# Two FFN layers on one core: the up-projection as seven half-size block products, and a down-projection that reads its input back from DRAM

## The chip, the cores and the metric

One Trainium2 chip, one of its cores. A core has TensorE (PE; its weight loads are listed as PEld), VectorE (DVE), ScalarE (ACT), GpSimd (POOL) and SyncE (SP, which only issues DMAs), each with its own in-order queue; they meet in semaphores. SBUF holds the working data in 128 partitions, PSUM is eight banks of 128 x 512 fp32, and DRAM is reached by DMA. The metric is the device time of one execution in microseconds (us); less is better.

## The reference

A two-layer encoder over 1024 prompt tokens and 256 sample tokens, all fp32, model width 1024. Layer 0 mixes tokens with a Conformer convolution, layer 1 with windowed attention; each mixer, and each FFN, is followed by a residual LayerNorm. The change touches the FFN and the normalisations on either side:

```
x = layer_norm(ALPHA * x + mix, ...)
h = depthwise_conv(x @ w_up, w_dw, b_dw)      # w_up 1024 x 5504, three taps along the tokens
g, u = split(h, 2)                             # gate and up, 2752 channels each
f = (silu(g) * u) @ w_down                     # w_down 2752 x 1024
x = layer_norm(ALPHA * x + f, ...)
```

## The kernel before

**Products.** Every fp32 operand is split into a high part (`fp32r`, a rounded copy) and a low part (what is left), and each product is three matmuls into one PSUM bank: high x high, low x high, high x low (`product`, L669, L672, L674). Weights come from DRAM in pieces of 128 x 512 (256 KB) into four slots (`raw_pieces`), and GpSimd makes both parts of each piece (L595, L599) in a ring of eight (`w_hi`, `w_lo`). A slot of the ring is written again when TensorE has used the piece that lay there.

**FFN.** The 2752 channels are 21 tiles of 128 (`FT` = 21) and a rest of 64. For each tile `up_tile(f)` computes 128 gate channels and 128 up channels in three token chunks (512, 512, 256): for each chunk and part, eight blocks of the contraction times three matmuls. So a tile is 96 matmuls of 512 columns and 48 of 256. ScalarE applies the centre tap on the way out of PSUM (L1275), VectorE the two others (L1606, L1612), ScalarE the silu (L1280), VectorE the product (L1625), and the two parts of h are made by ScalarE (L1287) and VectorE (L1639). h stays in SBUF, three tiles of it. After every second tile `down_pair(g)` multiplies the last two h tiles with their rows of `w_down`: 20 results of 128 tokens x 512, twelve matmuls for two, and VectorE adds each result to `y` in SBUF (L1645), 220 such additions a layer with the last tile and the rest. `up_rest` is the 64 + 64 left channels.

**Around it.** Before each FFN the output projection of the mixer runs in two halves of the columns, n = 0 and n = 1. While n = 1 runs token tile by token tile, VectorE adds and normalises each tile (L1568, L1393, L1406, L1411), TensorE turns it with eight transposes (L699), ScalarE makes its high part (L1130) and VectorE its low part (L1419), one tile behind another. At the end of the FFN `last_down(t)` gives each token tile its last ten matmuls, and VectorE then adds, normalises and splits the tiles one by one; in layer 0 the K and V projections stand between them, in layer 1 the tiles go out: VectorE L1700, ScalarE L1301, GpSimd L659, store by SP.

**Order.** There is no planner: each engine's program is written out, in the order of its queue.

Of the kernel before, what the change touches and what calls it, by code (L numbers as in the profile page):

```python
# [57 lines left out]
def trunk(nc, w, out_prompt, out_sample, residual_dram):  # L58
# [26 lines left out]
    GROUPS = (FT - 1) // 2  # L85
    assert 2 * GROUPS + 1 == FT and GROUPS % 2 == 0
    CONV_COLS = 2 * FT + 1

# [5 lines left out]
    UP_AT, DOWN_AT, N_FFN = [], [], 0  # L94
    for f in range(FT):
        if f >= 3 and f % 2:
            DOWN_AT.append(N_FFN)
            N_FFN += 4
        UP_AT.append(N_FFN)
        N_FFN += 4  # L100
    UP_AT.append(N_FFN)
    DOWN_AT += [N_FFN + 2, N_FFN + 6]
    N_FFN += 10
    assert len(DOWN_AT) == GROUPS + 1
    B_KV = B_FFN0 + N_FFN
    B_Q = B_KV + 8
# [3 lines left out]
    FFN_BASE = [B_FFN0, B_FFN1]  # L110

    with ExitStack() as ctx:
# [7 lines left out]
        XW = HW = T  # L120
# [6 lines left out]
        XL = sb("x_lo", [P, KT, XW], F32R)  # L127
        y = sb("y", [P, TT, D])
# [54 lines left out]
        OUT_AT = [0, HALF - 1, S0, T]  # L183
        OUT_MAX = HALF + 1
        with ExitStack() as a:
            h_first = [sb("h_hi_third", [P, HW], F32R, where=a), sb("h_lo_third", [P, HW], F32R, where=a)]
            HR = sb("h_rest", [P, HW], F32R, where=a)
            h_slot = [[sb(f"h_{part}_{i}", [P, HW], F32R, where=a) for part in ("hi", "lo")] for i in range(2)]
            g_conv = [sb(f"gate_conv{i}", [P, OUT_MAX], where=a) for i in range(2)]
            u_conv = [sb(f"up_conv{i}", [P, OUT_MAX], where=a) for i in range(2)]  # L190
            edge = sb("edge_columns", [P, 2, 2], where=a)
        HH, HL = ([h_slot[0][i], h_slot[1][i], h_first[i]] for i in range(2))
        with ExitStack() as a:
            gain = sb("gain_rows", [P, D], where=a)
            shift = sb("shift_rows", [P, D], where=a)
        with ExitStack() as a:
            sb("below_bias", [P, 3 * HW], where=a)
            pw2_bias = sb("pw2_bias_rows", [P, D], where=a)
# [52 lines left out]
        res_stored = sem("residual_stored")  # L251
# [3 lines left out]
        ffn_up = sem("ffn_up_done")  # L255
        ffn_mid = sem("ffn_centre_taps_done")
        ffn_edge = sem("ffn_edge_columns_kept")
        ffn_conv = sem("ffn_conv_done")
        ffn_gc = sem("ffn_gate_ready")
        ffn_silu = sem("ffn_silu_ready")  # L260
        ffn_prod = sem("ffn_product_ready")
        ffn_hi = sem("ffn_h_hi_ready")
        ffn_h = sem("ffn_h_ready")
# [1557 lines left out]
```

## Time and profile before

| | us |
|---|---|
| median of 3 runs | 2860.65 |
| lowest and highest of them | 2860.15, 2862.54 |
| profiled execution, first to last instruction (its span) | 2858.5 |
| TensorE busy in it | 2750.6 (96%) |
| VectorE busy | 1510.3 (53%) |
| GpSimd busy | 840.7 (29%) |
| ScalarE busy | 772.0 (27%) |

The profiled execution has no time of its own beside its span; the three runs lie 1.7 to 4.0 us above that span, the median 2.15 us. Busy time counts an engine as working from the start to the modelled end of its instructions. Matmuls overlap in the pipeline, so what a matmul costs is read from the distance between two starts and not from its own length. TensorE's granted clock was 0.988 of 2.4 GHz on average.

### The profile page before, as it was taken

The numbers are of one execution on the slowest core, as the hardware profiler recorded it, in microseconds if no ns is written. First come the engines' busy times: TensorE is split into PE (matmuls) and PEld (weight loads), VectorE is DVE, ScalarE is ACT, GpSimd is POOL, SyncE is SP. The second block draws the span as 40 slices with busy tenths as digits, with TensorE's granted clock in tenths as the row PEclk, the third lists the DMA queues.
The fourth block names the chain that finished last, engine by engine and source line by source line (L and its number), as shares of the span: only waits on it lengthen the run. The fifth ranks groups of instructions, "written<-read, shape, count | busy, mean of one in ns | idle before, by whom it ended". The sixth has DMA issues, their size and how long they took to land.

```text
span 2858.5 us, 36567 instructions
## 1 busy us (share of the span) xinstructions
PE 2750.6 (96%) x14349; PEld 2260.0 (79%) x14349; DVE 1510.3 (53%) x2542; ACT 772.0 (27%) x1791; POOL 840.7 (29%) x813
## 2 busy tenths in 40 slices
PE   8999869999999999999989999999999999999995
PEld 7887758788888888888778744778888888888884
DVE  3689865754444454434680288275444544444457
ACT  3333562221111122211221288213111222111122
POOL 3221202232232333223213166422323223232323
PEclk9999989999999999999999999999999999999998
DMA  4100003111111111111121000411111111111111
GB/s 138 30 23 22 30 1 125 30 45 34 41 45 30 45 37 41 39 33 45 58 82 45 0 1 1 152 33 37 39 36 45 37 38 37 37 45 30 45 37 74
DMA packets 158648, 124.69 MB, mean 44 GB/s; under 512 B 27906, under 2 KB 135802, under 8 KB 158489
## 3 DMA queue, kind: packets, MB, share of 16 engines
q1 hardware_dynamic: 149640, 96.83, 11.9%
q10 hardware_dynamic: 8848, 25.69, 2.5%
q8 instruction: 106, 1.74, 0.3%
q14 instruction: 54, 0.43, 0.1%
HBM read 112.01 MB, written 10.49 MB: 43 GB/s over the span
## 4 chain that ended last, share of the span: by engine, by line
PE 85%; DVE 10%; ACT 3%; issue 2%; DMA 0%; POOL 0%; POOLq 0%; DVEq 0%; ACTq 0%; SPq 0%
PE bank L669 26%; PE bank L672 25%; PE bank L674 25%; PE bank L754 3%; PE bank L1034 2%; PE bank L1050 2%; PE bank L1062 2%; DVE y L1482 2%; DVE stats L1393 1%; DVE y L1411 1%; ACT y L1244 1%; DVE y L1406 1%; DVE x_lo L1419 1%; DVE y L1645 1%; PE bank L699 1%
## 5 line engine op out<-in xcount | busy, mean ns | idle before, releaser
L669 PE MATMUL bank<-x_hi,w_hi 128*128 128x512 f32 (+1 forms) x2688 | 959.8, 357 | 3.7 <-DVE x_lo L1419 1.6
L674 PE MATMUL bank<-x_hi,w_lo 128*128 128x512 f32 (+1 forms) x2688 | 952.5, 354 | 0.0
L672 PE MATMUL bank<-x_lo,w_hi 128*128 128x512 f32 (+1 forms) x2688 | 952.3, 354 | 0.0
L595 POOL CAST w_hi<-raw_pieces 128x512 fp32r<-128x512 f32 x348 | 246.6, 709 | 1823.4 <-issue 1260.6
L669 PEld LDWEIGHTS bank<-x_hi,w_hi 128*128 128x128 f32 x2688 | 509.1, 189 | 90.3 <-issue 9.6
L674 PEld LDWEIGHTS bank<-x_hi,w_lo 128*128 128x128 f32 x2688 | 508.9, 189 | 71.0
L672 PEld LDWEIGHTS bank<-x_lo,w_hi 128*128 128x128 f32 x2688 | 509.3, 189 | 69.9
L599 POOL TENSOR_TENSOR w_lo<-raw_pieces,w_hi 128x512 fp32r<-128x512 f32 x348 | 469.4, 1349 | 27.9
L1645 DVE TENSOR_TENSOR y<-y,bank 128x512 f32<-128x512 f32 x440 | 296.2, 684 | 195.7 <-PE bank L674 193.8
L1606 DVE SCALAR_TENSOR_TENSOR gate_conv<-bank,ffn_conv_table,gate_conv 128x510 f32<-128x510 f32 x132 | 86.2, 653 | 372.9 <-ACT up_conv L1275 370.9
L669 PE MATMUL bank<-w_hi,h_hi 128*128 128x512 f32 x560 | 218.2, 390 | 3.3 <-DVE y L1645 3.3
L672 PE MATMUL bank<-w_lo,h_hi 128*128 128x512 f32 x560 | 218.0, 389 | 0.0
L674 PE MATMUL bank<-w_hi,h_lo 128*128 128x512 f32 x560 | 217.9, 389 | 0.0
L1482 DVE SCALAR_TENSOR_TENSOR y<-glu,conv_table,y 128x1024 f32 (+3 forms) x266 | 215.6, 883 | 0.1
L1270 ACT ACTIVATE edge_columns<-bank 128x2 f32<-128x2 f32 x86 | 14.8, 173 | 718.2 <-PE bank L674 718.2
L669 PE MATMUL bank<-w_hi,x_hi 128*128 128x512 f32 (+1 forms) x400 | 150.8, 377 | 17.3 <-DVE x_lo L1543 9.1
L1602 DVE SCALAR_TENSOR_TENSOR gate_conv<-edge_columns,ffn_conv_table,gate_conv 128x2 f32<-128x2 f32 x44 | 11.7, 265 | 266.4 <-ACT up_conv L1275 264.6
L1280 ACT ACTIVATE gate_conv<-gate_conv 128x511 f32<-128x511 f32 (+1 forms) x132 | 74.2, 562 | 283.3 <-DVE gate_conv L1612 270.0
L674 PE MATMUL bank<-w_hi,x_lo 128*128 128x512 f32 (+1 forms) x400 | 147.9, 370 | 0.0
L672 PE MATMUL bank<-w_lo,x_hi 128*128 128x512 f32 (+1 forms) x400 | 147.8, 369 | 0.0
L669 PEld LDWEIGHTS bank<-w_hi,h_hi 128*128 128x128 f32 x560 | 105.2, 188 | 25.5 <-issue 4.1
L674 PEld LDWEIGHTS bank<-w_hi,h_lo 128*128 128x128 f32 x560 | 105.1, 188 | 21.9
(175 smaller groups left out, 3416.2 us busy)
## 6 DMA issues: line engine op xcount, KB each, us to landing
raw_pieces<-in_ffn_w_up_dram SPq DMA_DIRECT2D x168, 256.0 KB, 2.8
raw_pieces<-in_ffn_w_down_dram SPq DMA_DIRECT2D x84, 256.0 KB, 2.6
raw_pieces<-in_conv_w_pw_dram SPq DMA_DIRECT2D x48, 256.0 KB, 2.7
y<-in_x_prompt_dram ACTq DMA_DIRECT2D x16, 512.0 KB, 7.0
residual_dram<-y ACTq DMA_DIRECT2D x10, 512.0 KB, 2.6
y<-residual_dram ACTq DMA_DIRECT2D x10, 512.0 KB, 12.2
out_dram<-y SPq DMA_DIRECT2D x10, 512.0 KB, 2.6
raw_pieces<-in_attn_w_q_dram SPq DMA_DIRECT2D x32, 128.0 KB, 2.4
```

Source lines behind the costliest of these rows:

```text
L595: pool.tensor_copy(WH[:, p % RING, :], raw[:, p % RAW, :]).then_inc(piece_hi, 1)
L599: pool.tensor_tensor(WL[:, p % RING, :], raw[:, p % RAW, :], WH[:, p % RING, :].bitcast(F32), ALU.subtract).then_inc(piece_split, 1)
L669: mm = pe.matmul(out, left[0], right[0], start=first, stop=False)
L672: pe.matmul(out, left[0], right[1], start=False, stop=False)
L674: return pe.matmul(out, left[1], right[0], start=False, stop=last)
L754: mm = pe.matmul(bank[b + h][:, 0:n], diagonals[left][rows], right[rows, at:at + n], start=(first and m == 0), stop=(last and m == 2))
L1034: pe.matmul(bank[SCORE_BANKS[q % 3]][:, 0:len(kb) * P], q_sb[half, GROUP * rr + s // 2, cols(n)], k_sb[half, rr, kb[0] * P:(kb[-1] + 1) * ...
L1050: mm = pe.transpose(bank[PROBS_BANKS[u % 3]][:, cols(r)], probs_of(i)[:, 2 * r + par, c0:c0 + P], ident[:])
L1280: act.activation(gb[0:rows, 0:n], gb[0:rows, 0:n], ACT.Silu).then_inc(ffn_silu, 1)
L1482: ins = dve.scalar_tensor_tensor(out=out, in0=glu[:, c, a0 + k:a0 + k + n], scalar=tap(k), in1=out, op0=ALU.mult, op1=ALU.add)
L1606: dve.scalar_tensor_tensor(out=bufs[part][:, to], in0=bank[2 * (s % 2) + part][:, at], scalar=tab(0, part), in1=bufs[part][:, to], op0=ALU ...
L1645: dve.tensor_tensor(y[:, t, half], y[:, t, half], bank[4 + m % 4][:], ALU.add).then_inc(down_kept, 1)
```

## The change

**Up-projection.** For the 1024 prompt tokens, each tile of 128 gate and 128 up channels is now a 2 x 2 block product. The left blocks are A11, A12 (tokens 0 to 511, first and second half of the 1024 inputs) and A21, A22 (tokens 512 to 1023); the right blocks are B11, B21 (gate) and B12, B22 (up). It is computed with seven products in place of eight: A11 B11, A12 B21, S2 T2, S3 T3, S1 T1, A22 T4, S4 B22, each of twelve matmuls of 512 columns. The S are sums of the token blocks, made once a layer by GpSimd in rows of `y` (`row_sums`, `last_row_sum`), then turned by TensorE in 32 "cells" of four transposes, with a high part by ScalarE and a low part by VectorE per cell. The T are sums of weight pieces, four additions a tile on VectorE (`weight_sums`). The seven products go to banks X, Y and W; between them ScalarE copies a bank out while the same bank goes on accumulating, and VectorE adds the rest (`sum_c11`, `sum_c22`, `sum_c21`). The 256 sample tokens are computed as before.

**h.** The convolution, silu and product now run on whole rows of 1280 tokens, and h goes to DRAM in fp32, one store a tile from ScalarE's queue.

**Down-projection.** After all tiles the down-projection runs for token tiles 0-3, 4-6 and 7-9 in turn. Each of these groups goes through all 22 steps of h and `w_down`, summed in PSUM, so `w_down` is loaded and split three times and VectorE adds to `y` 20 times a layer. The normalisation of one group stands beside the steps of the next.

**Splits.** In the FFN the high part of a weight piece is now made by ScalarE, the low part by GpSimd. The residual rows go to DRAM before the FFN and come back inside the down-projection.

The core of the diff:

```diff
+    ROLES = 8
+    D_GROUPS = [(0, 4), (4, 7), (7, TT)]
+    D_BANKS = [(4, 3, 2, 0, 7, 5, 1, 6), (4, 3, 2, 0, 5, 1), (4, 3, 2, 0, 5, 1)]
+    H_STEPS = FT + 1
+    H_RING = 4
...
+        h_dram = nc.dram_tensor("h_dram", (H_STEPS, P, T), F32, kind="Internal").ap()
...
+            def row_sums(layer, j):
+                pool.wait_ge(ln_ready, ln + j + 5)
+                pool.wait_ge(res_stored[j + 4], done)
+                pool.tensor_tensor(a21, a21, a22, ALU.add).then_inc(sums_ready, 1)
+                pool.wait_ge(res_stored[j], done)
+                pool.wait_ge(cell_turned, CELLS * layer + 2 * j + 2)
+                pool.tensor_tensor(a11, a21, a11, ALU.subtract).then_inc(sums_ready, 1)
+                pool.tensor_tensor(a12, a12, a11, ALU.subtract).then_inc(sums_ready, 1)
...
+                for j in range(3):
+                    row_sums(layer, j)
+                role_low(layer, 0, 0)
+                role_low(layer, 0, 1)
+                role_low(layer, 0, 2)
+                row_sums(layer, 3)
+                role_low(layer, 0, 3)
+                role_low(layer, 0, 4)
+                for j in range(4):
+                    last_row_sum(layer, j)
...
+                    def p6():
+                        pe.wait_ge(piece_split, p + 4)
+                        pe.wait_ge(up_kept, kept + 1)
+                        block(X, p + 3, S2, False, True, more=True, uses=1, ...).then_inc(ffn_x, 1)
+                    def p5():
+                        pe.wait_ge(piece_split, p + 6)
+                        pe.wait_ge(up_kept, kept + 2)
+                        block(X, p + 5, S1X, False, True, more=True, uses=1, ...).then_inc(ffn_x, 1)
+                    def p4():
+                        pe.wait_ge(piece_split, p + 7)
+                        pe.wait_ge(up_kept, kept + 3)
+                    def p3():
+                        pe.wait_ge(piece_split, p + 8)
+                        pe.wait_ge(up_summed, summed + 2)
...
+                        for part in (up_sample_low, p1, gate_sample_low, p2, gate_sample_high, p6, p7, p5, p4, p3,
+                                     up_sample_high):
+                            part()
...
+                def down_step(g, f):
+                    pe.wait_ge(h_low, H_ALL * layer + i + 1)
+                    for n in range(2):
+                        pe.wait_ge(piece_split, p + 1)
+                        for t in range(t1 - t0):
+                            if f == 0:
+                                down_bank_free(g, u)
+                            mm = product(out, (hi[:, cols(t)], lo[:, cols(t)]), weights, f == 0, False, uses=last)
...
+                def weight_sums(f):
+                    dve.wait_ge(piece_split, done + 2)
+                    dve.tensor_tensor(b11, b12, b11, ALU.subtract).then_inc(t_ready, 1)
+                    dve.tensor_tensor(t2_sum[:], b22, b11, ALU.subtract).then_inc(t_ready, 1)
+                    dve.tensor_tensor(b12, b22, b12, ALU.subtract).then_inc(t_ready, 1)
+                    dve.tensor_tensor(b21, b21, t2_sum[:], ALU.subtract).then_inc(t_ready, 1)
-                def add_down(m, t, n):
-                    dve.wait_ge(down_done, d0 + m + 1)
-                    dve.tensor_tensor(y[:, t, half], y[:, t, half], bank[4 + m % 4][:], ALU.add
```

**ScalarE in one tile in the middle of the up-projection.** Names: `edge_columns`, `gate_conv`, `up_conv` are buffers of one chunk; `gate_rows`, `up_rows` hold the sums of products, `gate_out`, `up_out` the convolved rows, `t_sum` one of the weight sums. Before, two of the three chunks:

```order
L1270 ACTIVATE edge_columns<-bank 128x2
L1275 ACTIVATE gate_conv<-bank,ffn_conv_table 128x511
L1270 ACTIVATE edge_columns<-bank 128x2
L1275 ACTIVATE up_conv<-bank,ffn_conv_table 128x511
L1280 ACTIVATE gate_conv<-gate_conv 128x511
L1287 ACTIVATE h_hi<-up_conv 128x511
L1273 ACTIVATE gate_conv<-edge_columns,ffn_conv_table 128x1
L1275 ACTIVATE gate_conv<-bank,ffn_conv_table 128x512
```

Now, from the first product's copy on:

```order
L1561 ACTIVATE gate_rows<-bank 128x512
L1511 ACTIVATE w_hi<-raw_pieces 128x512 x2
L1557 ACTIVATE gate_out<-bank,ffn_conv_table 128x256
L1592 DMA h_dram<-up_out 128x1280
L1511 ACTIVATE w_hi<-raw_pieces 128x512
L1561 ACTIVATE gate_rows<-bank 128x512
L1511 ACTIVATE w_hi<-t_sum 128x512
L1561 ACTIVATE up_rows<-bank 128x512
L1511 ACTIVATE w_hi<-raw_pieces 128x512 x3
L1557 ACTIVATE gate_out<-gate_rows,ffn_conv_table 128x1024
L1561 ACTIVATE up_rows<-bank 128x512
```

Eight weight copies, a store and four bank copies have come into ScalarE's queue; the bank copies stand behind weight copies that wait for ring slots.

**GpSimd at the start of a layer's FFN.** Before, the pieces of the first tile only:

```order
L595 CAST w_hi<-raw_pieces 128x512 [waits raw_landed3,piece_used]
L599 TENSOR_TENSOR w_lo<-raw_pieces,w_hi 128x512 [waits piece_hi]
L595 CAST w_hi<-raw_pieces 128x512 [waits raw_landed0,piece_used]
L599 TENSOR_TENSOR w_lo<-raw_pieces,w_hi 128x512 [waits piece_hi]
L595 CAST w_hi<-raw_pieces 128x512 [waits raw_landed1,piece_used]
L599 TENSOR_TENSOR w_lo<-raw_pieces,w_hi 128x512 [waits piece_hi]
```

Now, the last of the first three row sums and on (`t2_sum` is a weight sum):

```order
L732 TENSOR_TENSOR y<-y 128x512 [waits residual_stored6,ln_ready]
L736 TENSOR_TENSOR y<-y 128x512 [waits row_sums_ready,cell_turned,residual_stored2]
L738 TENSOR_TENSOR y<-y 128x512 [waits row_sums_ready]
L718 TENSOR_TENSOR w_lo<-raw_pieces,w_hi 128x512 [waits piece_hi] x3
L732 TENSOR_TENSOR y<-y 128x512 [waits residual_stored7,ln_ready]
L736 TENSOR_TENSOR y<-y 128x512 [waits row_sums_ready,cell_turned,residual_stored3]
L738 TENSOR_TENSOR y<-y 128x512 [waits row_sums_ready]
L718 TENSOR_TENSOR w_lo<-t2_sum,w_hi 128x512 [waits piece_hi]
L718 TENSOR_TENSOR w_lo<-raw_pieces,w_hi 128x512 [waits piece_hi]
L744 TENSOR_TENSOR y<-y 128x512 [waits row_sums_ready,cell_turned] x4
```

The low parts of the first pieces now stand behind nine additions that wait for the LayerNorm of token tiles 4 to 6 and for their stores.

## Rows read from the trace of the kernel before

**Rows 1.** The page: busy time; the chain that ended last, by engine.
```profile
PE 2750.6 (96%) x14349; PEld 2260.0 (79%) x14349; DVE 1510.3 (53%) x2542; ACT 772.0 (27%) x1791; POOL 840.7 (29%) x813
PE 85%; DVE 10%; ACT 3%; issue 2%; DMA 0%; POOL 0%; POOLq 0%; DVEq 0%; ACTq 0%; SPq 0%
```
**Rows 2.** Stretches: length, busy PE, PEld, DVE, ACT, POOL (count); clock, DMA share, GB/s.
```profile
474.70:574.90 100.20, 94.82 (x466) 79.16 (x465) 75.42 (x109) 19.78 (x42) 24.54 (x23) 0.97 0.11 29
574.90:1417.20 842.30, 839.72 (x4153) 713.52 (x4154) 387.45 (x624) 166.45 (x337) 244.88 (x245) 1.00 0.14 40
1417.20:1521.60 104.40, 92.06 (x564) 80.11 (x563) 68.73 (x119) 19.41 (x45) 23.82 (x24) 0.98 0.24 77
1859.30:1958.10 98.80, 93.38 (x466) 78.09 (x464) 70.22 (x105) 19.78 (x42) 24.35 (x23) 0.98 0.11 30
1958.10:2800.70 842.60, 839.95 (x4154) 713.67 (x4155) 387.72 (x624) 166.46 (x337) 240.81 (x240) 1.00 0.14 38
2800.70:2858.50 57.80, 27.11 (x99) 19.51 (x98) 46.24 (x71) 14.34 (x20) 23.64 (x10) 0.80 0.23 91
440.00:475.00 35.00, 33.95 (x151) 27.78 (x150) 16.50 (x16) 1.94 (x2) 14.27 (x14) 1.00 0.67 240
```
**Rows 3.** TensorE's timeline: start, length, line, what; first and last of a run.
```profile
630.37 0.40 PE L669 MATMUL bank<-w_hi,h_hi 128*128 128x512 f32 x1
...
679.13 0.39 PE L674 MATMUL bank<-x_hi,w_lo 128*128 128x512 f32 x1
679.36 0.28 PE L669 MATMUL bank<-x_hi,w_hi 128*128 128x256 f32 x1
...
684.99 0.28 PE L674 MATMUL bank<-x_hi,w_lo 128*128 128x256 f32 x1
...
552.10 1.04 PE L699 MATMUL bank<-ident,y 128*128 128x128 f32 x8
552.89 0.47 PE L669 MATMUL bank<-x_hi,w_hi 128*128 128x512 f32 x1
```
**Rows 4.** Groups by form: count, busy us, mean ns; idle before, releaser.
```profile
L599 POOL TENSOR_TENSOR w_lo<-raw_pieces,w_hi 128x512 fp32r<-128x512 f32 x348 | 469.4, 1349 | 27.9
L1645 DVE TENSOR_TENSOR y<-y,bank 128x512 f32<-128x512 f32 x440 | 296.2, 684 | 195.7 <-PE bank L674 193.8 <-PE bank L967 1.8
L1419 DVE TENSOR_TENSOR x_lo<-bank,x_hi 128x512 fp32r<-128x512 f32 x80 | 51.6, 686 | 69.7 <-ACT x_hi L1130 69.6
L1130 ACT ACTIVATE x_hi<-bank 128x512 fp32r<-128x512 f32 x80 | 43.2, 590 | 42.4 <-PE bank L699 42.4
L1625 DVE SCALAR_TENSOR_TENSOR up_conv<-gate_conv,up_conv 128x511 f32<-128x511 f32 x42 | 29.1, 692 | 5.0 <-ACT gate_conv L1280 0.5
```
**Rows 5.** TensorE's timeline behind an idle stretch.
```profile
542.11 1.97 PE L699 MATMUL bank<-ident,y 128*128 128x128 f32 x8 [4.71 <-DVE y L1411]
...
544.30 0.63 PE L672 MATMUL bank<-x_lo,w_hi 128*128 128x512 f32 x1
...
548.14 0.44 PE L672 MATMUL bank<-x_lo,w_hi 128*128 128x512 f32 x1
```
**Rows 6.** Timeline of VectorE and GpSimd: the same operations beside each other and alone.
```profile
539.96 2.09 DVE L1411 SCALAR_TENSOR_TENSOR y<-y,rstd,shift_rows 128x1024 f32<-128x1024 f32 x1
547.65 1.29 DVE L1411 SCALAR_TENSOR_TENSOR y<-y,rstd,shift_rows 128x1024 f32<-128x1024 f32 x1
538.85 2.12 POOL L599 TENSOR_TENSOR w_lo<-raw_pieces,w_hi 128x512 fp32r<-128x512 f32 x1
```
**Rows 7.** Timeline: GpSimd's last additions before the last store.
```profile
2850.83 4.64 POOL L659 TENSOR_TENSOR y<-y,shift_rows_end 128x1024 f32<-128x1024 f32 x2 [2.47 <-ACT y L1301]
```
**Rows 8.** DMA issues: what, queue, count, KB each, median us to landing.
```profile
raw_pieces<-in_ffn_w_down_dram SPq DMA_DIRECT2D x84, 256.0 KB, 2.6
residual_dram<-y ACTq DMA_DIRECT2D x10, 512.0 KB, 2.6
y<-residual_dram ACTq DMA_DIRECT2D x10, 512.0 KB, 12.2
```

More of the change, by code:

```diff
@@ L127, in trunk @@
         XL = sb("x_lo", [P, KT, XW], F32R)
+        with ExitStack() as a:
+            gate_out = sb("gate_out", [P, T], where=a)
+            up_out = sb("up_out", [P, T], where=a)
+            sb("below_sample", [P, 3 * D - 2 * T], where=a)
+            SMP = pair("sample", [P, KT, T - 2 * HALF], a)
         y = sb("y", [P, TT, D])
@@ L636, in normalise_part, with low, role_low @@
                 ins.then_inc(probs_ready_pool, 1)
-            def ffn_stretch(first, end):
-                for p in range(first, end):
-                    split(p, landed(p), p - RING + 1)
-                    split_low(p, p + 1)
+            def low(p, source):
+                pool.wait_ge(piece_hi, p + 1)
+                pool.tensor_tensor(WL[:, ring(p), :], source, WH[:, ring(p), :].bitcast(F32), ALU.subtract
+                                   ).then_inc(piece_split, 1)
+            def role_low(layer, f, j):
+                low(FFN_BASE[layer] + ROLES * f + j, role_source(RAW_BASE[layer] + 4 * f, j))
@@ new lines, in ffn, with block @@
+                x0, y0, w0, s0 = UPS_X * layer, UPS_Y * layer, UPS_W * layer, UPS_S * layer
+                kept0, summed0, cells0 = KEPT_ALL * layer, SUMMED_ALL * layer, CELLS * layer
+                tiles0 = FT * layer
+                def block(out, p, x, start, stop, uses=0, between={}, k0=0, more=False):
+                    for k in range(QUARTER):
+                        between.get(k, lambda: None)()
+                        mm = product(out, wblock(p, k), (x[0][:, k0 + k, :], x[1][:, k0 + k, :]),
+                                     start and k == 0, stop and k == QUARTER - 1, uses=uses and k == QUARTER - 1,
+                                     more=more)
+                    between.get(QUARTER, lambda: None)()
+                    return mm
@@ L982, in _ @@
+                for f in range(FT):
+                    sections(f)
+                rest()
+                for g in range(3):
+                    for f in range(H_STEPS):
+                        if layer == 0 and g >= 1 and f - 1 in LN_AT:
+                            t = D_GROUPS[g - 1][0] + LN_AT.index(f - 1)
+                            if t < D_GROUPS[g - 1][1]:
+                                turn_tile(1, t)
+                        down_step(g, f)
             unit = 0
@@ L1093, in _ @@
             out_projection(B_O, 1)
-            last_down = ffn(1, 3)
-            for t in range(TT):
-                last_down(t)
+            ffn(1)
         @block.scalar
```

1170 lines of the change are left out of this document (785 added, 385 removed).

## The prediction

> **What bounds the kernel now.** I read the page first: TensorE is busy for 96% of the span and carries 85% of the chain that ended last [rows 1]. So the time is the number of matmuls times the distance between two of them, plus the stretches in which TensorE waits. Then the stretches [rows 2]. In the two long ones, from the second up-tile of a layer to `last_down` (842.3 and 842.6 us), TensorE hardly waits. In the short ones it does: 10 to 17 us where a layer's FFN begins or ends, and 35 us at the very end, where PE is busy for 27.11 of 57.80. Last the timeline for the distances [rows 3]: 216 matmuls of 512 columns start from 630.37 to 679.13, 0.2268 us each; 48 of 256 columns from 679.36 to 684.99, 0.1198 each; eight transposes take 0.79.
>
> I write one block (4 x 3 matmuls of 512 columns) as 2.72 us. An up-tile before is 96 x 0.2268 + 48 x 0.1198 = 27.5 us.
>
> The sum is made against the span of the profiled execution, 2858.5 us. The median of the runs is 2.15 us above it, and I add that at the end.
>
> **1. The long stretches: 12 matmuls fewer a tile.** Seven blocks of twelve for gate and up over 1024 tokens in place of eight: an up-tile becomes 84 x 0.2268 + 48 x 0.1198 = 24.8 us. The rest of 64 channels (48 + 24 matmuls, 13.8 us) and the down-projection (1200 matmuls up to the last step's hundred, 272.2 us) keep their number. One long stretch had 20 x 27.5 + 13.8 + 272.2 = 836.4 us of work in 842.3. It will have 20 x 24.8 + 286.0 = 782.0.
>
> What hides the other engines' work in a tile of 24.8 us:
> - GpSimd: eight low parts at 1.35 = 10.8 [rows 4]; the high parts have gone.
> - ScalarE: eight weight copies and four bank copies at 0.59, then by the same rate per column three pieces of 1024 to 1280 columns and two of 256: about 12.
> - VectorE: four weight sums, three bank sums (0.69 each), two taps on 1023 columns for gate and up (some 1.3 each, as L1411 alone [rows 6]), sample taps, the product: about 14. The 220 additions into `y` (L1645, 0.684 [rows 4]) shrink to 20.
>
> None comes near 24.8, so the order within the queues decides. The tightest link: bank X is copied by ScalarE after S2 T2, and the next product into X, S1 T1, comes one block (2.72) later. ScalarE's queue holds nothing there that waits for anything later, and the copy takes 0.6, so some 1.9 us are spare. The same holds for W (A22 T4), and for the VectorE sum before S4 B22. Of the weight copies behind them each waits for a slot that TensorE frees one block later, and the piece it makes is wanted a tile afterwards. So I charge no wait a tile. If that cover goes, each of 40 tiles pays (rival A).
>
> Down-projection: a step is 24 matmuls (5.44 us) for four token tiles and 18 (4.08) for three. It needs two low parts from GpSimd (2.7), three copies from ScalarE (1.8), two weight pieces and one of h by DMA. ScalarE and GpSimd run up to three and a half steps ahead (ring of eight pieces, four of h). In SP's queue the h load of a step, which waits for h's low part four steps back, stands before the next rows; that also lies ahead of TensorE. The traffic is 512 KB + 192 KB in 4.08 us, about 175 GB/s. The stretch 440 to 475 moved 240 GB/s at a DMA share of 0.67 while TensorE was busy for 33.95 of 35 [rows 2]. The residual's return (ten loads that took 12.2 us each when issued together [rows 8]) falls in group 0. Bounds for waits in this stretch: 0 and 20 us a layer; before it was 6. I take 4, as it was nearly so before: 786.0.
>
> Two stretches: 1684.9 becomes 1572.0, **-112.9**.
>
> **2. Where a layer's FFN begins.** From the start of the n = 1 half to the second up-tile: 100.2 and 98.8 us [rows 2], of which 240 matmuls (54.4), the first tile (27.5) and 80 transposes (7.9) are work: 89.8. Now the first tile is 24.8, and 32 cells of four transposes are 12.6: work 91.8. The waits, from TensorE's arrival at the first product (57.6 in):
> - The low parts of pieces 0 and 1 stand behind nine row sums on GpSimd (1.3 each), the last three of which wait for the LayerNorm of token tile 6 (about 50 in; VectorE needs 4.3 for a tile, the additions and sums at 0.69 and two operations like L1411 at 1.2 to 1.3, and 1.4 for two cells) and for its store, issued only after the next tiles' deviations, 2.6 us to landing [rows 8]. They are ready at about 64.3: 6.7 us of wait.
> - The S3 cells want `last_row_sum`, behind three row sums and two low parts more: 9 x 1.3 after piece 1. TensorE arrives 4.5 us early.
> - Then VectorE paces: 24 low parts of cells (0.686 [rows 4]), two LayerNorms, seven sums, 30 us, before A22 T4 may begin. 5 us more.
> - The first pieces of the second tile wait for the end of the first: 1.
>
> Together 17. Some operations of VectorE and GpSimd stretch each other here: L1411 took 2.09 beside GpSimd and 1.29 alone, and a low part 2.12 [rows 6]. With 2 for that: 19 us of waits, where it was 10.4 and 9.0. 91.8 + 19 = 110.8, so +10.6 and +12.0: **+22.6**. Bounds: +3 a layer, if the stores and sums hide, and +25, if VectorE and GpSimd run at the stretched lengths all through.
>
> The Trainium skill ("GPSIMD Engine Reference", section Specifications) says that GpSimd's SBUF interfaces are shared with VectorE and contend when VectorE reads two SBUF inputs. By that rule the trace agrees with the 2.09 against 1.29. It speaks against this change, because the taps read `gate_rows` in SBUF now and not a bank; fully serialised, a tile would hold 10.8 + 9 us on that port, still under 24.8, so it would add nothing to a tile.
>
> **3. The end of layer 0.** 104.4 us [rows 2], with 100 matmuls of `last_down`, K and V (96 of 512, 288 of 256 columns) and 80 transposes: 86.9 of work. VectorE paced it, one LayerNorm and split after the other. Now tiles 0 to 6 are normalised beside the steps of later groups, only 7 to 9 are left, and K and V of the first chunk (19.4 us) stand before tile 7 is turned: VectorE has it by then. What is late next: in groups 1 and 2 a turned tile wants the low part of the one before, which VectorE makes within a microsecond of it. I take 3 us: 89.9, **-14.5**.
>
> **4. The end.** 57.8 us with 22.7 of matmuls. Now after the last step (2.7 us) comes for three tiles: add, statistics, gain (some 4 each), ScalarE's scale 1.15, GpSimd's addition 2.32, the last at about 19.9 from the start of that step, and 3.0 from GpSimd's end to the span's [rows 7]. So 22.7 + 20.2 = 42.9: **-14.9**.
>
> **Sum.** -112.9 + 22.6 - 14.5 - 14.9 = -119.7; 2858.5 - 119.7 + 2.15 = 2741 us.
>
> **Rivals.**
> A. The up-tile is paced by the exchange of banks between TensorE, ScalarE and VectorE. For it: three links of one block, and stretched VectorE operations [rows 6]. Against: 1.9 us spare. With 1.5 us a tile, 40 x 1.5 = 60: 2801. Chance 0.11.
>
> B. The first tile of a layer runs at the half clock. After 4.71 us idle, ten matmuls started 0.427 apart (544.30 to 548.14) [rows 5], the 1.2 GHz level, and this tile has a wait of 7 and several short ones. At that level all through, its 84 + 48 matmuls take 22.6 us more, of which some 7.6 fill waits: +15 a layer, 2771. Against: before, the full level was back at 548.4, and here the matmuls are dense between waits. Chance 0.12.
> The Trainium skill ("TensorE: Matmul & The Clock Gate", section What's actually happening) has the half rate as the default, released by activity; the rows 5 agree, and the rule would keep a stop-and-go tile slow.
>
> C. Slower than before: the down-projection is paced by its loads and splits. If the four raw slots and SP's order let only one step's pair be on its way, a step takes 2.6 (landing) + 0.6 + 2 x 1.35 + 0.4 = 6.3 us: 88 steps at +2.2 and 44 at +0.9 give 233: 2974. It outweighs the gain from 5.44 us a step in the groups of three, 132 GB/s. Against it: 240 GB/s in rows 2. Chance 0.05.
>
> D. The start hides as well as before (+3 a layer) and the long stretches have no wait: 2741 - 17 - 8 = 2716 to 2724. Chance 0.10.
>
> The forecast itself has 0.62, with 2728 to 2756 as its own range. That the change doesn't do what it says (more matmuls than counted) is excluded by the count of the blocks.
>
> The range, 2714 to 2802, reaches to D and A and leaves out C and what lies beyond these two. About 0.2% (6 us) is what a measurement can tell from no change. Faster 0.94, same 0.01, slower 0.05.
>
> **What would show it.** Right: TensorE's count down by 504 - 96 = 408; distances 0.2268 within a block; up-tiles 24.8 apart; down steps 4.08 and 5.44; no idle on TensorE beyond the layer's start. Wrong: idle time before a block with ScalarE's bank copy or VectorE's bank sum as releaser (A), granted clock under 0.9 in the first tile (B), idle before a down step with GpSimd's low part or a DMA as releaser (C).

## The result, and the profile after

The changed kernel takes 2762.8 us (median of 4 runs, 2762.3 to 2763.4) against 2860.4 (2859.8 to 2862.5) before on the same chip: 0.965 of it, with a 95% interval of 0.964 to 0.967. The forecast was 2741. The profiled execution has a span of 2761.5 us, 97.0 less than before, where the sum had 119.7.

The page of the changed kernel, busy time and the chain that ended last, beside [rows 1]:

```profile
PE 2650.4 (96%) x13941; PEld 2177.3 (79%) x13941; DVE 1524.8 (55%) x2112; ACT 1164.8 (42%) x2247; POOL 1217.5 (44%) x931
PE 86%; DVE 6%; ACT 3%; issue 2%; POOL 2%; DMA 1%; POOLq 0%; DVEq 0%; ACTq 0%; SPq 0%
```

The count of matmuls fell by exactly the 408 foreseen. GpSimd and ScalarE have half as much work again, and TensorE still carries the chain.

The same stretches as in [rows 2] (length, busy PE, PEld, DVE, ACT, POOL with counts; clock, DMA share, GB/s): a layer's FFN start, the rest up to the Q projection (two rows) or to the last matmul and the end, then a stretch of nothing but up-tiles and one of the down-projection:

```profile
476.58:593.13 116.55, 99.94 (x502) 81.25 (x500) 88.66 (x119) 31.19 (x60) 39.51 (x28) 0.96 0.19 68
593.13:1413.78 820.65, 815.50 (x4068) 692.61 (x4069) 436.74 (x472) 360.69 (x569) 430.36 (x307) 1.00 0.37 117
1413.78:1472.77 58.99, 58.99 (x409) 55.22 (x409) 19.98 (x45) 10.77 (x24) 10.67 (x12) 1.00 0.18 52
1812.37:1930.24 117.87, 100.92 (x501) 83.01 (x499) 83.77 (x115) 31.18 (x60) 38.30 (x28) 0.93 0.19 67
1930.24:2741.00 810.76, 807.10 (x4012) 685.84 (x4012) 411.52 (x452) 360.49 (x562) 429.23 (x301) 1.00 0.37 116
2741.00:2761.50 20.50, 0.00 (x0) 0.00 (x0) 10.66 (x17) 4.22 (x6) 6.99 (x3) 0.60 0.19 77
750.00:800.00 50.00, 50.00 (x267) 43.26 (x266) 28.87 (x33) 23.12 (x34) 22.61 (x16) 1.00 0.22 69
1140.00:1320.00 180.00, 178.39 (x801) 146.97 (x800) 79.70 (x79) 72.01 (x129) 108.56 (x78) 1.00 0.60 192
```

Each start is placed as in [rows 2], 16.4 us before the first eight transposes of the n = 1 half (those start at 492.94 and 1828.68 here, at 491.07 and 1875.61 before). Layer 0 from the n = 1 half to the Q projection takes 116.5 + 820.7 + 59.0 = 996.2 us, where it was 1046.9; layer 1 from the n = 1 half to the end 949.1, where it was 999.2. So 50.7 and 50.1 less. Of that the span lost 3.8 again in stretches that the change does not touch. The kernel's first batch of products took 17.0 us (17.01 to 34.02) where it took 15.0 (17.36 to 32.36), because the first of them were 0.43 apart as in [rows 5], the half clock (though the mean granted clock is given as 1.00 from 17.00 to 21.50). From the Q projection to layer 1's n = 1 half it took 339.6 us where it took 337.7; the mean granted clock from 1748 to 1753 was 0.66. Both differences are of these two profiled executions: in experiments 4, 5 and 6 the first batch took 15.0 again.

The layers themselves miss the forecast by 9.5 and 9.4 us, and most of it lies in the first row of each: 116.5 and 117.9 where 110.8 was expected.

TensorE's timeline there (start, length, line, what, idle before and releaser; layer 0, the rows with idle time), and the fifth prompt product of the second tile:

```profile
542.69 0.79 PE L803 MATMUL bank<-a_hi,w_hi 128*128 128x512 f32 x1 [7.50 <-POOL w_lo L718]
550.22 0.52 PE L848 MATMUL bank<-ident,y 128*128 128x128 f32 x3 [1.17 <-DVE s_lo L2025]
553.14 0.33 PE L848 MATMUL bank<-ident,y 128*128 128x128 f32 x1 [1.58 <-POOL y L744]
563.95 0.41 PE L848 MATMUL bank<-ident,y 128*128 128x128 f32 x2 [1.75 <-DVE s_lo L2025]
575.30 0.30 PE L848 MATMUL bank<-ident,y 128*128 128x128 f32 x1 [1.79 <-DVE a_lo L2025]
577.43 0.54 PE L803 MATMUL bank<-a_hi,w_hi 128*128 128x512 f32 x1 [1.50 <-DVE a_lo L2025]
593.13 0.39 PE L803 MATMUL bank<-sample_hi,w_hi 128*128 128x256 f32 x1 [0.81 <-POOL w_lo L718]
610.67 0.47 PE L803 MATMUL bank<-s_hi,w_hi 128*128 128x512 f32 x1 [1.97 <-ACT gate_rows L1561]
```

The seven waits up to the second tile add up to 16.1 us (16.9 in layer 1); 17 were forecast, in the same places, with 7.5 for 6.7 at the first product and 2.75 for 4.5 at the cells behind it. The stretch is 116.5 long with 91.8 of work, so 8.6 are left that no wait accounts for (9.2 in layer 1). These are matmuls further apart: the mean granted clock was 0.50 and 0.63 behind two of the waits (same columns), some 4 us in all, and the rest are fractions at 32 cells.

```profile
542.69:547.00 4.31, 4.31 (x15) 3.52 (x15) 3.76 (x3) 0.63 (x1) 4.14 (x3) 0.50 0.01 2
577.40:582.00 4.60, 4.57 (x17) 3.72 (x18) 1.17 (x2) 1.03 (x2) 0.00 (x0) 0.63 0.02 4
```

### The profile page after: what moved, and what is told of

It reads as the page before. It is cut to its first block, busy times and chain, and to the rows that moved or that the text cites. A ratio compares the mean times of both kernels' runs of the same rounds, so it can differ in the third digit from the quotient of the medians.

```text
span 2761.5 us, 37212 instructions
## 1 busy us (share of the span) xinstructions
PE 2650.4 (96%) x13941; PEld 2177.3 (79%) x13941; DVE 1524.8 (55%) x2112; ACT 1164.8 (42%) x2247; POOL 1217.5 (44%) x931
## 4 chain that ended last, share of the span: by engine, by line
PE 86%; DVE 6%; ACT 3%; issue 2%; POOL 2%; DMA 1%; POOLq 0%; DVEq 0%; ACTq 0%; SPq 0%
PE bank L803 25%; PE bank L806 25%; PE bank L808 25%; PE bank L902 3%; PE bank L1269 2%; PE bank L1285 2%; PE bank L1297 2%; DVE y L1924 2%; POOL w_lo L718 1%; ACT y L1473 1%; PE bank L833 1%; PE bank L848 1%; DVE y L1853 0%; DVE y L1848 0%; DVE stats L1834 0%
## 5 line engine op out<-in xcount | busy, mean ns | idle before, releaser
L718 POOL TENSOR_TENSOR w_lo<-raw_pieces,w_hi 128x512 fp32r<-128x512 f32 x564 | 787.9, 1407 | 737.2 <-ACT w_hi L1511 736.4
L1511 ACT ACTIVATE w_hi<-raw_pieces 128x512 fp32r<-128x512 f32 x564 | 351.3, 628 | 492.8 <-PE bank L803 414.5
L803 PE MATMUL bank<-s_hi,w_hi 128*128 128x512 f32 x680 | 268.0, 394 | 4.1 <-ACT gate_rows L1561 4.1
L806 PE MATMUL bank<-s_lo,w_hi 128*128 128x512 f32 x680 | 265.7, 391 | 0.0
L808 PE MATMUL bank<-s_hi,w_lo 128*128 128x512 f32 x680 | 265.4, 390 | 0.0
L803 PE MATMUL bank<-a_hi,w_hi 128*128 128x512 f32 x528 | 211.6, 401 | 18.0 <-POOL w_lo L718 15.0
L803 PE MATMUL bank<-x_hi,w_hi 128*128 128x512 f32 (+1 forms) x624 | 226.0, 362 | 1.6 <-DVE x_lo L1861 1.6
L808 PE MATMUL bank<-x_hi,w_lo 128*128 128x512 f32 (+1 forms) x624 | 221.5, 355 | 0.0
L806 PE MATMUL bank<-x_lo,w_hi 128*128 128x512 f32 (+1 forms) x624 | 221.3, 355 | 0.0
L806 PE MATMUL bank<-a_lo,w_hi 128*128 128x512 f32 x528 | 208.9, 396 | 0.0
```

Of the source, the lines that this page charges most:

```text
L718: pool.tensor_tensor(WL[:, ring(p), :], source, WH[:, ring(p), :].bitcast(F32), ALU.subtract).then_inc(piece_split, 1)
L803: mm = pe.matmul(out, left[0], right[0], start=first, stop=False, skip_group_check=more)
L806: pe.matmul(out, left[0], right[1], start=False, stop=False, skip_group_check=more)
L808: return pe.matmul(out, left[1], right[0], start=False, stop=last, skip_group_check=more)
L1511: act.activation(WH[:, ring(base + p), :], source, ACT.Copy).then_inc(piece_hi, 1)
```

## The experiments

All are edits of the changed kernel. Times are compared with its 2762.8, ratios with the kernel before on the chip of the run (for the changed kernel 0.9652).

**1. Eight blocks again**

```diff
-                        block(X, p + 7, S4, False, True, more=True).then_inc(ffn_x, 1)
+                        block(X, p + 7, S4, False, False, more=True)
+                        block(X, p + 7, S4, False, True, more=True).then_inc(ffn_x, 1)
```

> Each of the 21 up-tiles of a layer repeats its last prompt block, S4 B22, once more: 12 matmuls of 512 columns, so eight blocks a tile as before the change; loads, splits, copies and sums stay (h is then not the reference's). It takes back the term of the long stretches alone. My theory (TensorE bounds every tile, a block is 2.72 us): up-tiles 27.5 apart, +57.1 a layer, 2762.8 + 114 = 2877, TensorE still without idle time in the tiles. Rival 1 (TensorE is not all that paces the tiles; some of the saved block is filled by waits of other engines): less than +2.4 a tile, under 2863. Rival 2 (the wait at the fourth product of the second tile is hidden by the longer tile): 4 less, 2873.

Measured: 2874.9 us, ratio 1.0043 (1.0029 to 1.0057), 112 us more for 42 blocks; 2.67 a block. TensorE's sample products of two tiles stand 27.6 apart (708.32 and 735.90). No tile in the middle of the up-projection waits. The block is the whole gain: without it, the new structure is slower than the old one by 0.4%. The rows say where: in the changed kernel the two starts are 35.4 us longer than before, although each saves a block too, and the rest of the two layers is 27 us shorter than the saved blocks alone would make it.

**2. How far off the next bound is**

```diff
+                if two_pass[0]:
+                    return mm2
                 return pe.matmul(out, left[1], right[0], start=False, stop=last, skip_group_check=more)
```

> In the up-tiles from the second on and in the down-projection each product is two matmuls instead of three (high x low is left out, so the output is not the reference's); everything that other engines do stays. It shows how far off the next bound is. By count an up-tile would be 56 x 0.2268 + 32 x 0.1198 = 16.5 us, a down step 3.63 (four token tiles) and 2.72 (three). My theory: the up-tile follows TensorE down to 17 to 19 (GpSimd has 8 low parts at 1.35 to 1.41 = 11.3, VectorE 14.3, ScalarE 11.5 in it), the down steps of three stop at about 3.0, where GpSimd's two low parts (2.7 to 2.9) and 704 KB a step (the loads) are. Rival A (the exchange of banks or the copies pace the tile close under 24.8): 22 or more a tile. Rival C (the down-projection is near its bound by loads and splits): steps of three over 3.8, idle TensorE with a DMA or GpSimd as releaser.

Measured: 2465.4 us (one run). Up-tiles came 19.65 apart (first A11 B11 matmul at 659.33, 678.94, 698.64) with 16.5 of work. TensorE's timeline shows the two waits of a tile:

```profile
689.62 0.47 PE L804 MATMUL bank<-s_hi,w_hi 128*128 128x512 f32 x1 [1.27 <-ACT gate_rows L1568]
692.98 0.47 PE L804 MATMUL bank<-a_hi,w_hi 128*128 128x512 f32 x1 [1.28 <-ACT up_rows L1568]
```

and the timelines of VectorE and ScalarE what stands before them:

```profile
685.84 1.97 DVE L2119 SCALAR_TENSOR_TENSOR up_out<-gate_out,up_out 128x1280 f32<-128x1280 f32 x1
687.91 0.56 ACT L1564 ACTIVATE gate_out<-bank,ffn_conv_table 128x256 f32<-128x256 f32 x1 [4.53 <-DVE up_out L2119]
```

ScalarE waits 4.5 us for VectorE's product of the last tile, and the copies of banks stand behind that. So the next bound of an up-tile is the chain VectorE, ScalarE, bank, at 19.6 us, 5 under the 24.8 of TensorE. Rival A had the right place and the wrong distance. In the down-projection, steps of three token tiles ran at 2.72 in layer 0's group 1 (no idle in six steps from 1159.93 on); in layer 1 some waited 0.7 to 2.1 for GpSimd's low parts, where a GpSimd addition of 2.4 to 2.7 stood between. Layer 1's last group as a whole took 3.3 us a step (2370.28 to 2439.30, 21 steps). TensorE also waited up to 7.5 us for a turned tile in layer 0 and 8.8 at a change of group. A step of 4.08 is thus still clear of rival C, but by less than 2.72 says.

**3. Short row sums, and short low parts in layer 0's down-projection**

```diff
-                pool.tensor_tensor(a21, a21, a22, ALU.add)
+                pool.tensor_tensor(a21[:, 0:8], a21[:, 0:8], a22[:, 0:8], ALU.add)
...
+                pool.tensor_tensor(WL[:, ring(p), 0:8], raw[:, slot, 0:8], WH[:, ring(p), 0:8].bitcast(F32),
+                                   ALU.subtract).then_inc(piece_split, 1)
```

> Two edits in stretches that are apart. (1) GpSimd's 16 row sums a layer work on 8 columns instead of 512 (the S blocks are then not the reference's). (2) In layer 0's down-projection GpSimd's low parts are made for 8 columns only. Theory (the row sums in front of the first pieces' low parts are the wait of 7.5 us at the first product, and GpSimd stretches VectorE's operations with two SBUF inputs): the wait of 7.5 shrinks to under 2, the stretch from the n = 1 half to the second tile from 118 to 105 to 110 in both layers, so 2738 to 2748 in all; VectorE's low parts of h (128x384, 1.30 us on average) become about 0.5 in layer 0 and stay in layer 1. Rival (first tile is set by VectorE's chain of cells, LayerNorms and weight sums, or by the low clock): under 4 us a layer, 2755 or more; rival for (2): 1.30 is the operation's own length, and it stays in layer 0.

Measured: 2741.1 us, ratio 0.9575 (0.9559 to 0.9591), 21.8 us less. The first wait is 2.5 instead of 7.5, and the mean granted clock from 534 to 560 was 1.00 in place of 0.87. From the end of the n = 1 half to the second tile it took 48.6 us in place of 58.3, in layer 1 50.1 in place of 59.7. So the row sums cost 9.7 us a layer in that stretch. They are not the whole 21.8: from the fourth tile to the Q projection layer 0 was 3.4 us shorter, where its four waits of 0.8 had gone (three for a turned tile, one at a change of group). That belongs to the second edit, the short low parts. In layer 0's start no matmul ran at the half clock here, and 4.0 us still are neither work nor wait; that is the price of the handovers at the cells alone.

VectorE's low parts of h (by form, layer 0's groups of three while the down-projection ran) in the changed kernel, and then here in layer 0 and in layer 1:

```profile
L2124 DVE TENSOR_TENSOR h_lo<-h_raw,h_hi 128x384 fp32r<-128x384 f32 x42 | 55.2, 1314 | 78.4 <-ACT h_hi L1537 78.4
```

```profile
L2132 DVE TENSOR_TENSOR h_lo<-h_raw,h_hi 128x384 fp32r<-128x384 f32 x42 | 23.4, 558 | 114.0 <-ACT h_hi L1545 114.0
...
L2132 DVE TENSOR_TENSOR h_lo<-h_raw,h_hi 128x384 fp32r<-128x384 f32 x42 | 53.3, 1270 | 91.6 <-ACT h_hi L1545 91.6
```

The operation itself takes 0.56 us; beside GpSimd's full low parts it takes 1.3.

**4. The first wait filled with matmuls**

```diff
+                            for i in range(30):
+                                pe.matmul(X, A11[0][:, i % 4, 0:P], A11[0][:, i % 4, :], start=True, stop=True)
                         pe.wait_ge(piece_split, p + 2)
```

> In TensorE's wait of 7.5 us before the first product of a layer's FFN, 30 matmuls of 512 columns whose result is overwritten (6.8 us at the full clock) run; nothing else changes. It keeps TensorE busy over the wait and so tells the low clock from the wait. Theory (the idle time itself is what is lost, the low clock behind it costs some 2 us a layer): matmuls after the wait 0.2268 apart in place of 0.427, 1.5 to 3 us a layer less, 2757 to 2760. Rival B (the low clock in the first tile is most of the 8 us a layer that the start took over the forecast): 6 or more a layer, 2750 or less. Rival 3 (whatever TensorE saves, it waits for the cells' low parts instead): same, 2761 to 2763.

Measured: 2762.9, ratio 0.9651 (0.9634 to 0.9667): the same. The first wait was 0.81 and the matmuls behind it ran at the full distance, but the next cell then made TensorE wait 3.15 in place of 1.17, and behind that wait the matmuls were 0.43 apart:

```profile
539.95 0.50 PE L803 MATMUL bank<-a_hi,w_hi 128*128 128x512 f32 x1 [0.81 <-POOL w_lo L718]
547.49 0.45 PE L848 MATMUL bank<-ident,y 128*128 128x128 f32 x1 [3.15 <-DVE s_lo L2029]
...
548.80 0.63 PE L806 MATMUL bank<-a_lo,w_hi 128*128 128x512 f32 x1
549.23 0.63 PE L808 MATMUL bank<-a_hi,w_lo 128*128 128x512 f32 x1
```

So filling this wait gains nothing: TensorE only comes sooner to a cell that is not ready, and the low clock comes there instead. It does not show that the low clock is free, since it did not remove it. The same start, not edited up to its second tile, was profiled several times: from the end of the n = 1 half to the second tile it took 56.7 us with 8 matmuls of 512 columns at the half clock (experiment 5, layer 1), 58.3 with 11 and 59.7 with 15 (the changed kernel, layers 0 and 1), 60.2 with 19 (experiment 5, layer 0). The waits in it were 15.6, 16.1, 16.7 and 16.2. With the wait filled it was 60.0 with 17, and 59.6 with 13. The low clock costs a few us a layer and differs from one profiled execution to the next. Rival B had this cost right in kind, and too large: it took all 84 matmuls at the half clock.

**5. The second tile's queue order**

```diff
+                    if f > 1:
+                        next_high(f, 2)
                     keep_u2(f)
```

> In the second up-tile alone, ScalarE's copy of bank X after the second product into it (gate_rows, L1561) stands ahead of the weight copy next_high(1, 2), which waits for a DMA. Theory (the wait of 2.0 and 2.2 us at the fifth prompt product of the second tile is ScalarE's queue order, and the slow matmuls behind it the low clock): the wait goes, 2 to 4 us a layer, 2755 to 2759. Rival (the late loads of the third tile are the cause, and the wait moves to the next product or into the third tile): same, 2761 to 2764.

Measured: 2761.8, ratio 0.9652 (0.9638 to 0.9665): the same; the theory is refuted. The fifth product no longer waits; the sixth waits 2.46 for `up_rows`, which ScalarE copies behind the weight sum's high part. That comes late because the loads of the third tile's pieces do, and these wait for GpSimd's eight low parts of the second.

**6. Statistics in VectorE's gap**

```diff
-                weight_sums(0)
-                cells_low(8)
                 add_and_stats(8)
+                add_and_stats(9)
+                weight_sums(0)
+                cells_low(8)
```

> VectorE's additions and statistics of token tiles 8 and 9 stand ahead of the weight sums of the first tile, in the 6.5 us in which VectorE has nothing to do there (536.3 to 542.8 in layer 0), instead of between the cells. Theory (behind the first product VectorE's chain of cells, LayerNorms and sums paces TensorE; 2 x 2.2 us leave it): the waits of 1.75, 1.79 and 1.50 us shrink, 3 to 4.5 us a layer, 2754 to 2757. Rival 1 (GpSimd's row sums pace all of the first tile): same, 2761 to 2764. Rival 2 (VectorE is late for the weight sums by it and TensorE waits there): slower, 2764 to 2768.

Measured: 2761.5, ratio 0.9652 (0.9639 to 0.9665): the same. The waits stay, 1.67 and 1.80 and 1.50 where 1.75, 1.79 and 1.50 were. It did not separate the theories well: `norm_apply(9)` kept its place behind the cells of S4, and ScalarE's high part of the next cell waits 3.11 for exactly it.

**7. Three row sums given to VectorE, low parts sooner**

```diff
-                for j in range(3):
+                for j in range(2):
                     row_sums(layer, j)
                 role_low(layer, 0, 0)
                 role_low(layer, 0, 1)
+                row_sums(layer, 2)
                 role_low(layer, 0, 2)
-                row_sums(layer, 3)
...
+                row_sums_3()
                 weight_sums(0)
```

> The three row sums of j = 3 are VectorE's, in its idle stretch ahead of the weight sums; GpSimd makes the low parts of pieces 0 and 1 before the row sums of j = 2, and ScalarE makes their high parts ahead of the last deviation. Theory (GpSimd's row sums in front of the low parts are the wait of 7.5 us, and VectorE has room): the wait shrinks to 1 to 3 us, of which later waits give back some 2, so 3 to 5 us a layer less: 2752 to 2757. Rival (as with the filled wait, TensorE only arrives earlier at the next cell): under 1 us a layer, 2761 to 2763.

Measured: 2755.7, ratio 0.9631 (0.9617 to 0.9644): 3.5 us a layer, as expected, but not with room to spare. The first wait fell to 3.52 and the next cell's rose to 4.62. Of the 7.1 us between the medians, the two traces show 2.1 and 1.5 in the layers' starts up to the fourth tile, and 0.9 ahead of layer 0's, where nothing was edited. VectorE's three row sums and the first weight sum took 1.2 to 1.8 each while GpSimd worked, the three weight sums behind them 0.69, while it waited.

**8. The three together**

```diff
+                add_and_stats(8)
+                row_sums_3()
+                weight_sums(0)
+                add_and_stats(9)
```

> The three edits before it together; of the statistics, tile 8's stand ahead of the row sums and weight sums, tile 9's behind them. If the three savings add up as the theory has them (3, 3.5 and 4 us a layer): 2762.8 - 21 = 2742. If VectorE has no room for both the statistics and the row sums (rival): 2748 to 2754.

Measured: 2758.8, ratio 0.9643 (0.9630 to 0.9656): no better than the shared row sums alone, and above the 2748 to 2754 of the rival too. The savings do not add: in layer 0 the wait before the next cell was 5.69 in place of the 4.62 of experiment 7. That VectorE had no room is the likely reason; no run separates it from others.

**9. The LayerNorms of layer 1 not beside the steps**

```diff
-                    if tile_at(f) is not None:
+                    if layer == 0 and tile_at(f) is not None:
                         down_stats(g - 1, tile_at(f))
...
+                    for g in range(2):
+                        for t in range(*D_GROUPS[g]):
+                            down_stats(g, t)
+                            out_gain(t)
```

> In layer 1 alone, the statistics, gains, scales, shifts and stores of token tiles 0 to 6 (two groups) stand behind the last step's low part of h instead of beside the steps of the next group. It undoes the term of the end by itself. Theory (the end got shorter because VectorE has only three tiles left there; 4 us of VectorE a tile were hidden beside the matmuls and cost TensorE nothing): VectorE is free from 2728 on, seven tiles of 3.0 us take it to 2749, where the adds and tiles 7 to 9 begin 11 us later than now, so 2774 (2772 to 2776), and TensorE's last matmul stays where it is. Rival (the work beside the steps had slowed the steps themselves through ScalarE's, GpSimd's or SP's queue): the steps get shorter, and less than 8 us are lost, under 2771.

Measured: 2782.0, ratio 0.9722 (0.9707 to 0.9737): 19.2 us more, where 11 were expected. TensorE's steps were as before, so the rival falls and the LayerNorms beside the steps are free. The size missed, because a tile took VectorE 4.9 us and not 3.0. VectorE's and GpSimd's timelines:

```profile
2739.39 3.28 DVE L2143 SCALAR_TENSOR_TENSOR y<-y,mean_var,gain_rows_end 128x1024 f32<-128x1024 f32 x1
...
2739.25 2.34 POOL L779 TENSOR_TENSOR y<-y,shift_rows_end 128x1024 f32<-128x1024 f32 x1 [2.54 <-ACT y L1738]
```

In the changed kernel, with GpSimd idle:

```profile
2742.67 1.29 DVE L2143 SCALAR_TENSOR_TENSOR y<-y,mean_var,gain_rows_end 128x1024 f32<-128x1024 f32 x1 [0.47 <-DVE mean_var L1837]
```

The stretched one ends 1.08 us after GpSimd's addition ended (2741.59), nearly its whole length alone. In [rows 6] L1411 too ended 1.08 after GpSimd's low part beside it (542.05 and 540.97), after an overlap of 1.0 us where it was 2.2 here. An operation that only ran slower would have had less left to do after the longer overlap; it waited.

**10. The first tile in order of need**

```diff
-                for j in range(2):
-                    row_sums(layer, j)
+                row_sums(layer, 0)
                 role_low(layer, 0, 0)
                 role_low(layer, 0, 1)
+                row_sums(layer, 1)
+                role_low(layer, 0, 2)
                 row_sums(layer, 2)
...
-        tile, half, block_of = {2: (j, 0, S2), 3: (j, 0, S3), 4: (j + 4, 0, S1X), 5: (j, 1, S4),
+        tile, half, block_of = {2: (j, 0, S2), 3: (j + 4, 0, S1X), 4: (j, 0, S3), 5: (j, 1, S4),
...
+                weight_sums(0)
+                cell_low(8)
+                row_sums_3()
```

> On top of the shared row sums: GpSimd makes the low parts of pieces 0 and 1 behind the row sums of j = 0 and the others between the next ones; the cells of S1 are turned in the second product and those of S3 in the third; ScalarE copies the cells of S2 before the pieces 3 and 4; VectorE makes the weight sums ahead of its row sums, and the LayerNorm of tile 8 moves behind the cells of S3. Theory (TensorE waits in the first tile for the chain GpSimd, VectorE, cells; with the order by need the first wait goes and the 4.6 us before the third product shrink to 2, one of 2 comes before the fourth): 3 to 5 us a layer less than with the shared row sums alone, 2746 to 2750. Rival (the sum of GpSimd's and VectorE's work sets the end of the chain, whatever the order): 2754 to 2757. Rival 2 (the S3 cells, turned late, stop the fourth product): over 2757.

Measured: 2754.1, ratio 0.9626 (0.9613 to 0.9639). That is inside the rival's 2754 to 2757: TensorE starts the first product at once, and waits 5.36 before the third cell of S2, for GpSimd's row sum. The order moves the waits and takes little from their sum: from the n = 1 half to the second tile it took 113.1 and 114.2 us, with the shared row sums alone 115.4 and 116.5.

**11 and 12. One or both last additions on VectorE**

```diff
-            for t in range(*D_GROUPS[2]):
+            for t in range(D_GROUPS[2][0], TT - 1):
                 add_shift(t)
+                    dve.wait_ge(out_normed, TT)
+                    dve.tensor_tensor(y[:, TT - 1, :], y[:, TT - 1, :], shift_end[:], ALU.add).then_inc(last_ready, 1)
```

The second moves tile 8's too.

> On top of the reordered cells: the last addition of the shift, that of token tile 9, is VectorE's instead of GpSimd's; tile 8's stays on GpSimd and runs at the same time. Alone such an addition of 1024 columns should take VectorE about 1.25 us (two of the 512-column kind at 0.68, less one start), GpSimd 2.34. Theory of exclusion (an operation of VectorE that reads two SBUF inputs does not run beside one of GpSimd's, it waits for its end, as 3.27 beside 1.28 us in the late norms): VectorE's addition starts when ScalarE is done but ends only after GpSimd's of tile 8, so it takes 2.0 to 2.7 us, and the end comes 1 us earlier: 2753. Rival (each is slowed somewhat but they overlap): 1.3 to 1.6 us for it, the end 2 to 2.5 us earlier: 2751.7.

> The same, with the additions of tiles 8 and 9 both on VectorE, so that nothing of GpSimd's is beside them. Both theories: each about 1.25 us, the last one starts when ScalarE's scale of tile 9 is done; the span's end behind TensorE's last matmul 21.4 us now, 19 us then, so 2751.7 in all.

Measured: 2752.9 for both, ratios 0.9623 (0.9610 to 0.9636) and 0.9619 (0.9605 to 0.9632). From TensorE's last matmul to the end it took 21.2 us with the cells reordered, 20.2 with one addition moved, 19.1 with two. VectorE's last addition beside GpSimd's, from the timelines of both engines of the first:

```profile
2745.31 2.43 DVE L2290 TENSOR_TENSOR y<-y,shift_rows_end 128x1024 f32<-128x1024 f32 x1 [2.32 <-ACT y L1752]
...
2744.31 2.35 POOL L788 TENSOR_TENSOR y<-y,shift_rows_end 128x1024 f32<-128x1024 f32 x1 [2.54 <-ACT y L1752]
```

and both of them on VectorE, with nothing beside them:

```profile
2745.41 2.36 DVE L2291 TENSOR_TENSOR y<-y,shift_rows_end 128x1024 f32<-128x1024 f32 x2 [1.28 <-ACT y L1752]
```

Alone 1.22 each (the two overlap a little in this row); beside GpSimd it ended 1.08 after GpSimd's end (2746.66). Exclusion, not a slower rate. The second move made the tail 1.1 us shorter, but the median did not follow (2751.7 was expected): in its profiled execution the kernel's first batch of products was again 1.5 us longer than in that of experiment 11. The last version is 9.9 us under the changed kernel by the medians, and its ratio's interval lies below: the best of this study.

## Why the prediction was right, and where its sizes were off

The mechanism and the main term held; the total was less well met than the wide range suggests. 2762.8 lies 7 us above the forecast's own 2728 to 2756, which had a chance of 0.62, and none of the rivals came as described. Of the 22.7 us by which the sum was off, 12.8 lie in the two starts, 3.7 in the rest of layer 0, 2.4 in the rest of layer 1, and 3.8 in stretches outside the change.

**Term 1, the block: right.** The up-tiles are 24.9 us apart (first sample products at 744.85 and 769.71), TensorE is busy for 50.00 of 50, and experiment 1 gives the 112 us back. From the second tile on layer 0 took 879.6 us up to the Q projection where 875.9 was forecast, layer 1 809.9 up to the end of the last matmul where 808.7 was: layer 0's waits are the second tile's 2.0 with slow matmuls behind it, three of 0.8 for a turned tile and one of 0.8 at a change of group.

**Term 2, the start of the FFN: the mis-sized term.** Forecast 110.8 a layer, measured 116.5 and 117.9. The waits themselves were right (16.1 and 16.9 against 17, first among them 7.5 against 6.7 for the low parts behind the row sums). What failed is the last step, "With 2 for that" for stretched operations and no price for the clock and the handovers: matmuls further apart took 8.6 and 9.2. The trace of before had already shown such a loss. The prediction called all of 10.4 and 9.0 us there waits, but TensorE's idle times in those rows add up to 5.3 in either layer (4.7 of it the wait in [rows 5]); the rest was distance. The largest single cause in the stretch is the row sums: taking them out gives 9.7 us a layer, 5 to 7 of it in waits and the rest in distances. They cost twice, as GpSimd's own time and as time in which VectorE may not read two inputs from SBUF. The gap in which VectorE looked free was not worth much, as experiments 7, 8 and 10 show: two engines that exclude each other are one engine.

**Term 3, the end of layer 0: right.** 59.0 us without any idle time from 1413.78 on. **Term 4: nearly.** The tail from the last step's start is 24.1 where 22.9 was forecast; experiment 9 shows that the LayerNorms beside the steps are what made it short, and that they cost the steps nothing.

**The rivals.** A (banks): no wait in a tile; the slack is 5 us a tile, with the bound where A put it. B (clock): the low clock is there, 0.50 and 0.63, in short pieces, 11 and 15 matmuls of 512 columns a layer where B had 84; filling the first wait moved it and gained nothing. C (down-projection slower): refuted, 178.4 busy of 180 at 192 GB/s. D (start hides as before): refuted, TensorE waits 16 us there.

The Trainium skill's rule of shared SBUF interfaces ("GPSIMD Engine Reference", Specifications), weighed for the up-tile, added nothing there, as said; its price came in the first tile. The trace agrees, and shows the form of it: one operation waits for the end of the other (experiments 9 and 11). The half rate as the default, in the Trainium skill under "TensorE: Matmul & The Clock Gate", What's actually happening, also agrees with the matmuls 0.43 apart behind the waits.

What stays open: how much of the starts' excess is the low clock and how much the handovers, beyond the 4.0 us that were left in experiment 3's layer 0 without any slow matmul; what decides how long the low clock lasts from one execution to the next; and how much of VectorE's and GpSimd's time would be left if the row sums were made from PSUM; that was not tried.

## What to carry to other kernels

Count what a change removes from the busiest engine, then test it by putting exactly that back: one doubled block told the 112 us of gain from 12 us of loss that the rest of the rewrite brought. Before work is moved to an "idle" engine, look whether operations of the two stretch when they overlap; if they exclude each other, add their times. Filling a wait to keep the clock up gained nothing where the next thing was not ready: the wait and the low clock both moved on to it. And place the bounds of a stretch by its instructions before you compare it with another trace: 1.9 us of the first batch's slow products would otherwise have counted as the change's.

## What the runs showed of the hardware

- An operation of VectorE with two inputs in SBUF and one of GpSimd's exclude each other: 3.28 in place of 1.29 us (1024 columns), 2.43 in place of 1.22 (1024 columns, addition), 1.31 in place of 0.56 (384 columns). Operations of VectorE with one input in PSUM did not stretch: the low parts of cells took 0.69 beside GpSimd's additions and alone.
- It works both ways: GpSimd's low parts and additions of 512 columns took 1.3 alone and 1.5 to 2.3 beside such operations of VectorE.
- TensorE's half clock behind waits differs between executions of the same code: 8 to 19 matmuls of 512 columns 0.43 apart in a layer's first tile, and 15.0 or 16.3 to 17.9 us for the kernel's first batch of products.
